# Ten of eleven up-projection chunks as seven half products each, with weight sums made by adding DMAs

## The reference, cut to what matters

```python
def conv_ffn(xn, w_up, conv_w, conv_b, w_down):      # xn 512x1024, w_up 1024x5632
    val, gate = jnp.split(xn @ w_up, 2, axis=-1)      # two times 512x2816
    gc = conv_b + sum over j of conv_w[j] * gate shifted by 2 - j tokens
    return (jax.nn.silu(gc) * val) @ w_down           # 2816x1024
```

## Time and profile before

| what | us |
|---|---|
| median of 3 runs (2288.18 to 2293.38) | 2289.28 |
| span of the profiled execution | 2287.9 |
| PE busy, share of the span | 2236.4, 98% |
| DVE busy | 1255.1, 55% |
| ACT busy | 990.6, 43% |
| POOL busy | 360.9, 16% |
| moved by DMA | 236.7 MB, 103 GB/s |

### The profile page before, as it was taken

The page is one execution under the profiler, slowest core; times in us unless marked ns, Lnnn a source line. Parts: engine busy times, 40 slices in busy tenths (PEclk is TensorE's granted clock), DMA queues, the critical chain, the costliest instruction groups (busy, mean ns, idle before and its releaser), DMA issues.

```text
span 2287.9 us, 30159 instructions
## 1 busy us (share of the span) xinstructions
PE 2236.4 (98%) x11479; PEld 1806.6 (79%) x11479; DVE 1255.1 (55%) x2250; ACT 990.6 (43%) x1835; POOL 360.9 (16%) x432
## 2 busy tenths in 40 slices
PE   7899999999999999999989999999999999999999
PEld 6677777788877787878878888888888668888887
DVE  6966565756645454544493555464444565454543
ACT  7445655533554545463432423333344664232322
POOL 7742131126202030300000000000034000000000
PEclk9999999999999999999999999999999999999999
DMA  7354212134232222225462232322222302322232
GB/s 224 118 170 129 74 56 93 43 105 157 101 112 68 87 80 87 86 71 176 164 213 89 78 111 79 106 92 85 100 92 92 130 20 74 111 92 93 93 101 83
DMA packets 184559, 236.70 MB, mean 103 GB/s; under 512 B 29565, under 2 KB 110932, under 8 KB 184418
## 3 DMA queue, kind: packets, MB, share of 16 engines
q1 hardware_dynamic: 160462, 207.73, 28.1%
q10 hardware_dynamic: 23956, 27.04, 3.7%
HBM read 215.84 MB, written 23.10 MB: 104 GB/s over the span
## 4 chain that ended last, share of the span: by engine, by line
PE 88%; DVE 7%; ACT 2%; issue 1%; POOL 1%; DMA 1%; SPq 0%; ACTq 0%; DVEq 0%; POOLq 0%
PE G L2211 25%; PE G L2213 25%; PE G L2212 25%; DVE w_lo L1762 1%; PE X L2220 1%; PE X L2331 1%; PE X L2342 1%; PE X L2319 1%; PE X L2358 1%; PE X L2345 1%; PE G L2365 1%; PE G L2379 1%; PE X L2315 1%; PE X L2230 1%; POOL small L1172 1%
## 5 line engine op out<-in xcount | busy, mean ns | idle before, releaser
L2211 PE MATMUL G<-w_hi,u_hi 128*128 128x512 f32 x1536 | 622.5, 405 | 4.0 <-issue 2.1
L2213 PE MATMUL G<-w_hi,u_lo 128*128 128x512 f32 x1536 | 601.2, 391 | 0.0
L2212 PE MATMUL G<-w_lo,u_hi 128*128 128x512 f32 x1536 | 599.8, 391 | 0.0
L1762 DVE SCALAR_TENSOR_TENSOR w_lo<-raw,par,w_hi 128x512 fp32r<-128x512 f32 x496 | 373.6, 791 | 402.5 <-ACT w_hi L1250 399.6
L1250 ACT ACTIVATE w_hi<-raw,par 128x512 fp32r<-128x512 f32 x496 | 318.2, 714 | 342.3 <-PE G L2213 339.2
L2211 PE MATMUL G<-u_hi,w_hi 128*128 128x512 f32 (+1 forms) x1168 | 458.2, 392 | 0.3 <-DVE w_lo L1762 0.2
L2213 PE MATMUL G<-u_hi,w_lo 128*128 128x512 f32 (+1 forms) x1168 | 446.0, 382 | 0.0
L2212 PE MATMUL G<-u_lo,w_hi 128*128 128x512 f32 (+1 forms) x1168 | 445.8, 382 | 0.0
L2211 PEld LDWEIGHTS G<-w_hi,u_hi 128*128 128x128 f32 x1536 | 289.1, 188 | 70.1 <-issue 8.7
L2213 PEld LDWEIGHTS G<-w_hi,u_lo 128*128 128x128 f32 x1536 | 288.8, 188 | 62.3
L2212 PEld LDWEIGHTS G<-w_lo,u_hi 128*128 128x128 f32 x1536 | 289.5, 188 | 59.2 <-issue 1.9
(11 more groups left out here) (315 smaller groups left out, 2334.4 us busy)
## 6 DMA issues: line engine op xcount, KB each, us to landing
raw<-in_ffn_w_up SPq DMA_DIRECT2D x88, 512.0 KB, 4.7
raw<-in_e_w_in SPq DMA_DIRECT2D x56, 512.0 KB, 4.7
raw<-in_o_w_in SPq DMA_DIRECT2D x56, 512.0 KB, 4.5
raw<-in_ffn_w_down SPq DMA_DIRECT2D x40, 512.0 KB, 4.3
raw<-in_e_w_out SPq DMA_DIRECT2D x16, 512.0 KB, 4.6
raw<-in_o_w_out SPq DMA_DIRECT2D x16, 512.0 KB, 4.2
raw<-in_a_w_glu SPq DMA_DIRECT2D x16, 512.0 KB, 4.9
raw<-in_w_kv SPq DMA_DIRECT2D x16, 512.0 KB, 4.7
```

Source lines behind the costliest of these rows:

```text
L1762: V.scalar_tensor_tensor(w_lo[:, n % HL, k], raw[:, n % RAW, k], gain(name, k0 + k), w_hi[:, n % HL, k].bitcast(F32), ALU.mult, ALU.subtract)\
L2211: pe.matmul(out, lh, rh, start=start, stop=False)
L2212: pe.matmul(out, lh, rl, start=False, stop=False)
L2213: return pe.matmul(out, ll, rh, start=False, stop=stop)
```

## The change: what it does, and the diff

Ten of the eleven up chunks of each feed-forward (the stage `seven`) are made by the Strassen-Winograd scheme. Tokens are split in two halves of 256, input rows in two halves of 512, and output columns in two: the 256 gate and the 256 value columns. Seven half products (`PRODUCTS`) take the place of eight: each has 256 tokens, 512 input rows and 256 columns, that is two row blocks by four slices by three parts, 24 matmuls that stream 256 columns. Sums and differences of the quarters are needed on both sides:

- of the tokens (S1 to S4): POOL makes them once per feed-forward in `pool_token_sums`, eight 128x1024 additions, and ACT and DVE split them;
- of the weights (T1 to T4): POOL issues DMAs from memory to memory, four plain copies and four adding ones per layer, each in four row blocks of 128 rows by 2560 columns (1.31 MB), 64 DMAs in all, into a new memory tensor `dW`. One is issued at the end of POOL's iteration n for each n of `sum_units`: 32 to 37, 42 to 77, 82 to 89, 114 to 123 and 128 to 131. Each waits for the one before it;
- of the products: four additions by DVE and four copies by ACT out of PSUM for each chunk.

SP loads half units of 512 KB, seven for each chunk, in place of four; ACT splits each in one 128x1024 copy, DVE in one 128x1024 subtraction, through a ring of four half buffers in `w_hi` and `w_lo`. The gain `ffn_norm` is no longer a scale of the weights: it is loaded as rows and multiplied into the tokens by DVE's norm scaling. The first up chunk stays as it was but for that. `n % HL` becomes `wb[n]` and `4 * n` becomes `bb[n]` everywhere, with the same meaning.

```diff
+SEVEN = 10
+PRODUCTS = (("A11", "B11"), ("A12", "B21"), ("S1", "T1"), ("S2", "T2"), ("S4", "B22"), ("A22", "T4"), ("S3", "T3"))
...
+        SUMS = (("T1", "B11", False), ("T3", "B12", False), ("T1", "B12", True), ("T3", "B22", True),
+                ("T2", "T1", False), ("T2", "B22", True), ("T4", "T2", False), ("T4", "B21", True))
+        sum_jobs = [(layer, k, r) for layer in range(2) for k in range(len(SUMS)) for r in range(4)]
+        sum_units = [n for n in range(state["e_down"].n, NU)
+                     if n not in seven and not any(last - 1 <= n <= last + 2 for last, _ in tails)]
...
+            def seven_loads(s):
+                for q in range(7 * SEVEN):
+                    j, p = divmod(q, 7)
+                    name = PRODUCTS[p][1]
+                    if j:
+                        sp.wait_ge(*at_("sw_done", s.i, q - 7))
+                    elif name in MADE:
+                        if name == "T1":
+                            sp.wait_ge(sums_made, 16 * (s.layer + 1) * len(SUMS) * 4)
+                            sp.wait_ge(*at_("u_ready", s.norm.i, TT - 1, 1))
...
+                    sp.dma_start(weight_half(s, name), half_source(s.layer, j, name)).then_inc(half_loaded[p], 16)
...
+            def pool_weight_sum(i):
+                layer, k, r = sum_jobs[i]
...
+                if i:
+                    pool.wait_ge(sums_made, 16 * i)
+                if onto:
+                    pool.dma_start(dst, src, accum_op=ALU.add, max_dma_last_dim=5120).then_inc(sums_made, 16)
+                else:
+                    pool.dma_start(dst, src, max_dma_last_dim=5120).then_inc(sums_made, 16)
...
                 for last, s in tails:
                     if n == last:
                         pool_h_rms(s)
+                if n in seven and n == seven[n].n:
+                    pool_token_sums(seven[n])
+                if n in sum_units[:len(sum_jobs)]:
+                    pool_weight_sum(sum_units.index(n))
...
+                    if s.rows is not None:
+                        dve.wait_ge(rows_loaded, 16 * (s.rows + 1))
+                        V.scalar_tensor_tensor(xn_view[:, t, :], h[:, t, :], rstd[:, t:t + 1], row_scale,
+                                               ALU.mult, ALU.mult).then_inc(*by("xn_ready", s.i, t))
+                        continue
                     V.tensor_scalar(xn_view[:, t, :], h[:, t, :], rstd[:, t:t + 1], None, ALU.mult)\
...
+            def product_high(s, q):
+                act.wait_ge(*half_at(s, q))
+                act.wait_ge(blocks, s.base + q - 3 if q >= 4 else bb[s.n - 2] + 4 * (q // 2) + 4)
+                nc.scalar.activation(w_hi[:, r, :, c], weight_half(s, name), ACT.Copy)\
+                    .then_inc(*by("sw_high", s.i, q))
...
+            def dve_seven(s):
+                for q in range(7 * SEVEN):
+                    j, p = divmod(q, 7)
+                    product_low(s, q + 2)
+                    if q == 0:
+                        token_low(s, "S3")
+                    if j and p == 0:
+                        seven_late_half(s, j - 1)
+                    if j and p in (1, 3):
+                        seven_conv(s, j - 1, p // 2)
...
+            def pe_seven(s):
+                for q in range(7 * SEVEN):
...
+                    pe.wait_ge(*at_("sw_done", s.i, q))
...
+                    for m in range(2):
+                        o = slice(c.start + m * P, c.start + (m + 1) * P)
+                        for k in range(4):
+                            ins = three(b[:, 256 * m:256 * m + 256], (w_hi[:, r, k, o], w_lo[:, r, k, o]),
+                                        (x[0][:, k, :], x[1][:, k, :]), p in (0, 1, 2, 5) and m == 0 and k == 0,
+                                        m == 1 and k == 3, onto=p in (3, 4, 6))
+                    ins.then_inc(blocks, 1)
```

More of the change, by code:

```diff
@@ L114, in __init__ @@
                  wtype=None, nu=0, to=None, step=1, stage_at=0, hd=0, dst=0, layer=0, host=None, host_at=0, host_end=0, h_from=None,
-                 tail=None, lead=None, mem=None, x=None, more=None, more_at=0, ahead=None):
+                 tail=None, lead=None, mem=None, x=None, more=None, more_at=0, ahead=None, seven=None, rows=None):
         self.kind, self.src, self.name, self.T, self.n, self.h, self.y, self.kt = kind, src, name, T, n, h, y, kt
@@ L122, in __init__ @@
         self.tail, self.lead, self.mem, self.x = tail, lead, mem, x
-        self.more, self.more_at, self.ahead = more, more_at, ahead
+        self.more, self.more_at, self.ahead, self.seven, self.rows = more, more_at, ahead, seven, rows
 class Counts:
@@ L773, in build @@
         sems = {name: sem(name) for name in counts.total}
-        NUSED = sum(s.nu for s in plan if s.kind in ("down", "chunk"))
-        lo_pieces = [u[-1][1].stop for u in units]
+        NUSED = sum(s.nu for s in plan if s.kind in ("down", "chunk", "seven"))
+        seven = {s.n + u: s for s in plan if s.kind == "seven" for u in range(s.nu)}
+        lo_pieces = [0 if n in seven else u[-1][1].stop for n, u in enumerate(units)]
         lo_before = [sum(lo_pieces[:n]) for n in range(NU + 1)]
-        hi_pieces = [1 if g is None else 4 for g in unit_gain]
+        hi_pieces = [0 if n in seven else 1 if g is None else 4 for n, g in enumerate(unit_gain)]
         hi_before = [sum(hi_pieces[:n]) for n in range(NU + 1)]
@@ L791, in build @@
         rowwise = {s.n + s.nu - 2 for s in plan if s.kind in ("down", "chunk") and s.tail is not None}
+        bb, wb, done_blocks, buffer = [], [], 0, 0
+        for s in plan:
+            if s.kind in ("chunk", "down"):
+                for _ in range(s.nu):
+                    bb.append(done_blocks)
+                    wb.append(buffer)
+                    done_blocks, buffer = done_blocks + 4, 1 - buffer
+            elif s.kind == "seven":
+                s.base, s.first = done_blocks, buffer
+                bb += [done_blocks] * s.nu
+                wb += [None] * s.nu
+                done_blocks, buffer = done_blocks + 7 * SEVEN, 1 - buffer
@@ new lines, in quarter, with half_source @@
+        def quarter(layer, name):
+            k, c = {"B11": (0, 1), "B12": (0, 0), "B21": (1, 1), "B22": (1, 0)}[name]
+            o = DFF * c + 256
+            return w["ffn_w_up"][layer][SEQ * k:SEQ * k + SEQ, o:o + 256 * SEVEN]
+        def half_source(layer, j, name):
+            v = dW[layer, MADE[name]] if name in MADE else quarter(layer, name)
+            return v.rearrange("(k p) n -> p k n", p=P)[:, :, 256 * j:256 * j + 256]
+        sevens = [s for s in plan if s.kind == "seven"]
@@ L871, in build @@
         last_h = [s for s in plan if s.kind == "down"][-1]
+        row_norms = [(last + 1, s) for last, s in tails if s.rows is not None]
+        row_scale = att[:, 12:14, :].rearrange("p a n -> p (a n)")
         mem_view = att[:, 8:12, :].rearrange("p (t a) n -> p t (a n)", t=2)
@@ L1249, in w_high @@
                 for k in ks:
-                    nc.scalar.activation(w_hi[:, n % HL, k], raw[:, n % RAW, k], ACT.Copy, scale=gain(name, k0 + k))\
+                    nc.scalar.activation(w_hi[:, wb[n], k], raw[:, n % RAW, k], ACT.Copy, scale=gain(name, k0 + k))\
                         .then_inc(w_hi_done, 1)
@@ L1672, in _ @@
                             w_high(n + 2)
+                        if s.seven is not None:
+                            for q in ((0, 1), (2,))[u]:
+                                product_high(s.seven, q)
                 elif s.kind == "forget":
@@ L1683, in y_high @@
                             return
-                        act.wait_ge(blocks, 4 * (s.n + max(s.free_at[l] + 1, 0)))
+                        if s.seven is not None:
+                            act.wait_ge(*at_("s_y", s.seven.i, s.loads[l][-1] // 2 - 1))
+                        act.wait_ge(blocks, bb[s.n + max(s.free_at[l] + 1, 0)])
                         if s.hosted and l == len(s.groups) - 1:
@@ L1691, in _ @@
                     for p in range(s.nu):
+                        if s.seven is not None and p == 0:
+                            seven_silu(s.seven, SEVEN - 1)
                         for m in range(4 if p < s.hosted else 0):
@@ L2056, in _ @@
                             w_low(s.n + b // 4 + 1, ((0,), (1,), (2, 3))[b % 4])
+                        if s.seven is not None and b >= 4:
+                            if b % 2 == 0:
+                                product_low(s.seven, b // 2 - 2)
+                            if b != 6:
+                                token_low(s.seven, {4: "S1", 5: "S2", 7: "S4"}[b])
                         if s.host is not None and s.host is not prep:
@@ L2171, in _ @@
                                 add_h(0, m)
+                            if s.seven is not None and (p, m) in ((0, 2), (0, 3)):
+                                seven_conv(s.seven, SEVEN - 1, m - 2)
+                            if s.seven is not None and (p, m) == (1, 0):
+                                seven_y(s.seven, SEVEN - 1)
```

(1 more changed line is left out.)

335 lines of the change are left out of this document (287 added, 48 removed).

## The result

The changed kernel takes 2388.6 us (4 runs, 2384.5 to 2391.5) against 2288.7 us for the kernel before on the same chip: 1.0434 times as long, 95% interval 1.0418 to 1.0451. It is slower by 100 us, where 29 were forecast. The profiled execution has a span of 2385.3 us, 97.4 more than the 2287.9 before.

The account below looks back on a forecast made before the run. PE was taken as the bound, busy for 98% of the span. The terms -32.0 + 50.8 + 5 + 5 = +28.8 us on the 2289.3 median gave 2318 us, range 2264 to 2372.

Parts of the forecast that it names:

- Part 1: PE's products in the seven stage: 20.16 us a chunk for 21.76 before, over 20 chunks 32.0 us off.
- Part 2: ACT, DVE, SP and POOL's token sums beside the products: all fit within a chunk's 20.16 us, zero cost.
- Rival 3: DVE becomes the bound of the new stage: 22 us a chunk, 2355 us with the stalls; chance 0.09 with other delays.
- Part 3: Edges of the seven stage: 2.5 us lost per feed-forward, 5 in all, ends 0 and 10.
- Part 4: Weight-sum transfers in POOL's queue: 19 waits ahead of three groups' masks and the odd layer's norm, 50.8 us of stalls.
- D: Mean time of POOL's transfers from issue to landing, taken as 7.1 us; stalls = 19 x D - 84.
- Part 5: S5 layer: eight transfers beside DMA engines already 0.70 busy, 5 us lost, ends 0 and 20.
- Rival 1: POOL's transfers quick enough, D under 5.6 us, so the kernel gets faster: 2261 to 2284 us; chance 0.27.
- Rival 2: POOL's transfers slow, 11.6 us per copy: 2354 us at D = 9, over 2400 at 11.6; chance 0.14.

Follow-up runs that it names:

- e11: e9 with POOL's eight token additions per feed-forward replaced by memory sets (other numbers in the products): 2263.6 us, ratio 0.9894.
- e4: Changed kernel with POOL's eight token additions replaced by tiny memory sets (other numbers in the products): 2374.1 us, ratio 1.0365.
- e9: e8 with the first layer's transfers of units 32 to 37, 42 and 43 moved to units 70 to 77: 2279.7 us, ratio 0.9962.
- e6: Changed kernel with the last whole chunk's convolution, SiLU and products put ahead of half tiles and token sums on ACT and DVE: 2374.0 us, ratio 1.0365.
- e8: Changed kernel with transfers moved to other units, one per unit, plus e6's entry order and e3's later token sums: 2300.3 us, ratio 1.0049.
- e3: Changed kernel with POOL's token sums started only when DVE has split the last whole unit: 2388.1 us, ratio 1.0426.
- e7: Changed kernel with no transfers in units 80 to 91, the second layer's running up to unit 139 instead: 2361.9 us, ratio 1.0319.
- e1: Changed kernel without the 64 transfers, plain weight quarters read in place of sums: 2288.2 us, ratio 0.9999.
- e12: e9 without the 64 transfers, plain weight quarters read in place of sums: 2276.3 us, ratio 0.9945.
- e2: Changed kernel with each transfer waiting only for the one of its own row block, four back: 2367.1 us, ratio 1.0335.
- e10: e9 with POOL joining the halves of A11 and A12 before the wait for the last whole unit's split: 2272.9 us, ratio 0.9934.

## Why the prediction was wrong

The sign and the main mechanism were right. The time, 2388.6, lies outside the range of 2264 to 2372, and the change cost more than three times what was forecast. The profiled spans differ by 97.4 us against 28.8 forecast, 68.6 too little:

- **Part 1 (products, -32.0) was right.** Matmuls in the stage are 120.0 ns apart, as forecast, a chunk takes 20.16 us for 20.16, and e11 shows 32.1 us in the two feed-forwards (365.05 - 349.08 and 362.65 - 346.49). The 47 us estimated from the Trainium skill (TensorE: Matmul & The Clock Gate, section Back-to-back issue gap) don't come out; the page gives that formula for a single isolated matmul and not for a stream of them.
- **Part 2 (ACT, DVE, SP beside the products) was right for the stage**, with 14.5 of 20 us of DVE, and the DMA share without transfers beside it (1560 to 1600 us) is 0.59 for 0.57. Rival 3 is out. ("By the same measure" ACT's copies of 512 would be 0.48 and not 0.6; they take 0.58, and nothing hangs on it.) **Its last sentence, the token sums at zero, is the first step that failed.** It asked only whether POOL would be ready in time. It didn't ask what POOL's adds do to DVE beside them. Without them the two feed-forwards together are 17.9 us shorter in the old order (e4) and 16.9 in the new one (e11 against e9).
- **Part 3 (edges, 5) failed for the same stretch.** The prediction says that the first low parts stand behind sums of tokens, but I took 2.5 us without writing down the order of ACT, DVE and SP there. The order is worth 16.3 us (e6). It and the adds are partly the same loss: alone they give 16.3 and 17.9, together 28.6. Parts 2 and 3 together: 5 forecast, 32.1 - 3.5 = 28.6 measured, 23.6 of the 68.6.
- **Part 4 (POOL's waits, 50.8) was right in kind, and near in size at the three groups.** D was taken as 6.8 for a copy and 9.6 for an adding transfer. Over the whole kernel the 32 copies land after 6.6 us in the median (5.6 to 10.3) and the 32 adding ones after 11.3 (9.3 to 15.2); the 9.9 of the issues that read the input mixes both kinds. Cut at POOL's rms steps, the three groups lost 16.7, 17.2 and 15.2 us for 13.5, 15.6 and 14.5 forecast, and the norm 14.4 for 7.2. At the norm the term that was too small is D itself: the four waits, all for copies, took 34.8 us from issue to issue (550.54 to 585.30), 8.7 each and not 6.8, and 34.8 less 20.0 to spare is 14.8, nearly what was lost. Over all 19 waits D was (34.8 + 37.2 + 36.5 + 34.0) / 19 = 7.5 for 7.1. The 20 us of e8 are the same sum again: 43 us in front of the rms less 20.0 to spare. The memory layer's chunk lost 8.5, for which I had said zero to 5 with the stick-breaking layer (4.9) together. Together 76.9 for at most 55.8; half of the 26 us missing from 50.8 is 8.5 + 4.9 at places that I had not worked out.
- **Part 5 (S5, 5, up to 20) failed in size:** 24.0, and 29.7 to 30.5 in e3, e4 and e6. I had the row, 0.70 of the DMA engines busy with PE waiting for loads, and eight transfers of 1.31 MB, each reading and writing, on top of it. The share went to 1.01, the layer's own 256 KB transfers landed after 9.4 and 9.6 us for 4.1 and 3.9, and PE stood behind them. e7 confirms it from the other side: without the eight transfers the layer takes 180.8 us. Against the forecast that is 19.0 more, part 4 is 26.1 more and the entry 23.6: together 68.7, the whole of what was missing.
- **Rival 1** (quick transfers, by the Trainium skill's fit: 5.0 us) is out: copies take 6.6, adding transfers 11.3, and the mean of the 19 waits, 7.5, is above the 5.6 at which it would have won. **Rival 2** (slow transfers) is nearer in time but not what happened: the five waits of the first group take (795.59 - 758.41) / 5 = 7.4 us each, not 9. At D = 9 it had 2354 us; the measured time is beyond that for other reasons, the entry and the S5 layer.

A rule of the Trainium skill should have been weighed and wasn't: SBUF — State Buffer, section Who interferes with whom, says that a VectorE instruction with two SBUF inputs contends with a GpSimd instruction that reads SBUF, through a shared read interface, and that the contention is an exclusive lock. The trace agrees: splits of some 0.7 us from two SBUF tiles take 2.6 us, about one of POOL's adds of 2.7 each, while DVE's convolution out of PSUM at 1420.14, with POOL adding from 1416.7 to 1422.5, takes 0.80, as before.

What stays open: the stick-breaking layer is 0.5 to 0.6 us longer than before without transfers or with four chains (e1, e12, e2) and 1.9 to 5.1 in the kernels of the table with transfers one at a time, which points to POOL's waiting again; which of its tasks is late there is not shown. Nor was it tried to make the token sums on another engine.

## What to carry to other kernels

Put a wait for a slow transfer into an engine's queue only where that engine's next task has more time to spare than the transfer takes. The same 64 transfers cost 100 us in front of masks and beside a load-bound stage, and 3 us where POOL has time to spare and the loads beside them are asked for early. For a new stage, write out the order of each engine from the last old task to the first new one: a steady gain of 16 us was nearly all lost in an entry of 45 us. Work on POOL isn't free because POOL is idle: ask which of DVE's operations run beside it.

## What the runs showed of the hardware that was not expected

- Beside POOL's 128x1024 float32 adds (2.7 us), DVE's 128x512 subtractions of two SBUF tiles take 2.6 us in place of some 0.7, and 128x1024 ones 2.1 to 3.4 in place of 1.22.
- Memory-to-memory transfers of 1.31 MB issued by POOL land after 6.6 us in the median as copies and after 11.3 as adding ones; beside the half-unit loads in e10 that is 5.9 to 9.2 and 11.8 to 14.1. Four at a time, those that read the input land after 17.5 in the median.
- With the DMA engines at 0.96 to 1.05 and one transfer in flight, the steady part of a stage whose loads are asked for a chunk ahead shows no gap of PE. The entry of the same stage with four in flight does (e2: 1.02, PE busy for 5.1 of 20 us). The S5 layer, whose 256 KB transfers are waited for one after the other, does so at 1.01 with one: they land after 9.4 and 9.6 us for 4.1 and 3.9.
